# Wide products with an unread result on TensorE, around the first transposes and in the router stage of a hybrid decoder layer

## The reference, cut to what matters

```python
def decoder_layer(h, p, conv_prev, ssm_prev, prm):
    mix, ... = token_mixers(rmsnorm(h, g_mix), conv_prev, ssm_prev, prm)   # w_in, convolution, scan, chunk mix, w_out
    h = h + mix
    m = rmsnorm(h, g_moe)
    h = h + moe(m, ...)                     # 32 experts
    gate = sigmoid(rmsnorm(h, g_ple) @ w_ple_gate)
    return h + (p @ w_ple_proj) * gate, ...

def moe(x, ...):
    logits = x @ w_router + b_router
    top_v, top_i = top_k(logits, 4); gates = softmax(top_v)
    # for every expert e, on the rows that chose it:
    #   u = x[rows] @ w_up[e] + b_up[e]           1024 -> 2048
    #   act = gate * sigmoid(1.702 * gate) * (lin + 1)
    #   out[rows] += (act @ w_down[e] + b_down[e]) * g      1024 -> 1024
```

## Time and profile before

| | us |
|---|---|
| three runs, median (lowest, highest) | 1175.32 (1175.0, 1187.63) |
| profiled execution, its own time | 1171.86 |
| span of its profile | 1170.1 |
| TensorE busy | 1105.9 (95%) |
| TensorE weight loads | 454.9 (39%) |
| VectorE busy | 387.0 (33%) |
| ScalarE busy | 142.4 (12%) |
| GpSimd busy | 33.9 (3%) |
| HBM read | 429.04 MB |

### The profile page before, as it was taken

How to read it: one execution, slowest core, us unless ns; L and a number is a source line. 1 busy time by engine, 2 the same in 40 slices (tenths; PEclk the granted TensorE clock), 3 DMA queues, 4 the chain that set the end, 5 groups by cost and what they waited for, 6 DMA issues and landing times.

```text
span 1170.1 us, 16352 instructions
## 1 busy us (share of the span) xinstructions
PE 1105.9 (95%) x6482; PEld 454.9 (39%) x6482; DVE 387.0 (33%) x979; ACT 142.4 (12%) x318; POOL 33.9 (3%) x81
## 2 busy tenths in 40 slices
PE   5999999999999999989898899999989898989896
PEld 5746356333333433333333233334333333333332
DVE  3727656322222231313131122233223132222255
ACT  1322213100000100000000100001010000000022
POOL 2300021000000000000000000000000000000000
PEclk9999998999999999999999999999999999999999
DMA  8833194899999999999999999999999999999941
GB/s 285 269 148 114 42 388 182 348 429 427 428 426 426 428 428 427 429 428 428 430 427 428 427 429 426 427 428 428 428 429 428 427 428 428 429 429 429 425 179 41
DMA packets 42334, 433.88 MB, mean 371 GB/s; under 512 B 6691, under 2 KB 7851, under 8 KB 17720
## 3 DMA queue, kind: packets, MB, share of 16 engines
q1 hardware_dynamic: 40224, 428.74, 87.6%
q0 software_dynamic: 1488, 4.48, 1.1%
q10 hardware_dynamic: 584, 0.14, 0.1%
HBM read 429.04 MB, written 4.30 MB: 370 GB/s over the span
## 4 chain that ended last, share of the span: by engine, by line
PE 71%; DMA 26%; DVE 1%; ACT 1%; issue 1%; SPq 0%; DVEq 0%; ACTq 0%
PE bank L971 27%; DMA ring<-in_w_up_dram 25%; PE bank L1017 12%; PE bank L955 6%; PE bank L611 5%; PE bank L707 4%; PE bank L637 3%; PE bank L939 3%; PE bank L1001 1%; PE bank L593 1%; PE bank L1046 1%; PE bank L936 1%; PE bank L1007 1%; PE bank L870 1%; PE bank L812 1%
## 5 line engine op out<-in xcount | busy, mean ns | idle before, releaser
L971 PE MATMUL bank<-ring,aT 128*64 128x512 f32 x1536 | 350.0, 601 | 28.8 <-DMA ring<-in_w_up_dram 27.7
L971 PEld LDWEIGHTS bank<-ring,aT 128*64 128x64 f32 x1536 | 106.8, 138 | 255.7 <-issue 201.0
L1017 PE MATMUL bank<-ring,arena 128*64 128x512 f32 x768 | 169.6, 594 | 0.2
L1795 DVE TENSOR_TENSOR h<-h,bank 128x512 f32<-128x512 f32 (+1 forms) x96 | 65.7, 684 | 178.2 <-PE bank L955 175.9
L971 PE MATMUL bank<-arena,aT 128*64 128x512 f32 x512 | 115.6, 596 | 3.4 <-DMA arena<-in_w_up_dram 3.4
L1812 DVE TENSOR_SCALAR arena<-bank 128x256 f32<-128x256 f32 x64 | 27.2, 425 | 238.7 <-PE bank L971 237.4
L1821 DVE COPY aT<-bank 64x512 f32<-64x512 f32 x32 | 22.2, 694 | 245.0 <-PE bank L1017 245.0
L1271 ACT ACTIVATE arena<-arena 128x256 f32<-128x256 f32 x64 | 26.7, 417 | 548.6 <-DVE arena L1812 548.6
L1017 PEld LDWEIGHTS bank<-ring,arena 128*64 128x64 f32 x768 | 53.8, 137 | 100.9 <-issue 98.2
L955 PE MATMUL bank<-aT,arena 128*128 128x512 f32 (+1 forms) x192 | 83.5, 622 | 1.4 <-DVE aT L1821 0.9
L971 PEld LDWEIGHTS bank<-arena,aT 128*64 128x64 f32 x512 | 35.3, 136 | 77.6 <-issue 69.9
(11 more groups left out here) (313 smaller groups left out, 758.6 us busy)
## 6 DMA issues: line engine op xcount, KB each, us to landing
ring<-in_w_up_dram SPq DMA_DIRECT2D x96, 2048.0 KB, 32.6
ring<-in_w_down_dram SPq DMA_DIRECT2D x48, 2048.0 KB, 33.2
arena<-in_w_up_dram SPq DMA_DIRECT2D x32, 2048.0 KB, 33.0
arena<-in_w_down_dram SPq DMA_DIRECT2D x16, 2048.0 KB, 33.6
ring<-in_w_in_dram SPq DMA_DIRECT2D x3, 2048.0 KB, 14.1
ring<-in_w_in_dram SPq DMA_DIRECT2D x4, 1024.0 KB, 8.6
ring<-in_w_out_dram SPq DMA_DIRECT2D x1, 4096.0 KB, 13.0
ring<-in_w_ple_gate_dram SPq DMA_DIRECT2D x2, 2048.0 KB, 13.4
```

The costliest lines, as they stand in the source:

```text
L971: mm = pe.matmul(bank[n][CAP * hf:CAP * hf + CAP, :], xT[:, odd, 2 * j + a, :], up_cols(x, j, a, hf, n), start=False, stop=(j == 3 and a = ...
L1017: mm = pe.matmul(bank[4][CAP * hf:CAP * hf + CAP, :], actT[:, b, t, :], tile_of(x, UP_TILES + t)[:, 1024 * b + 512 * hf:1024 * b + 512 * h ...
L1795: tt(part, part, bank[5 + j % 2][at:at + ROWS[c], :], ALU.add).then_inc(s_free[j % 2], 1)
```

## The change

A new view `idle_rows` covers 256 float32 columns of the arena, read as 512 bf16 columns. VectorE's first instruction sets it to zero and gives `idle_ok`. A new helper `keep_clock(n, b, rows)` issues n products of a 128 by 128 bf16 stationary operand with 512 bf16 columns, each with start and stop, into bank b. No engine reads these results; where the bank is used later, its first product has start set, so it writes over them. There are 24 such products before the parameter turns, 10 before the first transposes and 2 after each of the six transposing jobs, all on zeros; then 2 before the last logits, 3 between L912 and L914, 2 before the wait for `sel0_ok` 2, and 4 after L925, on the normed rows `parts_0`. Before the first of these router groups two waits are added, for the store of the transposes of row group 1's first half and for `m1_ok` 2, which ScalarE gives when it has written those normed rows.

```diff
@@ -173,6 +173,7 @@
         bsn = view(11008, P)
         lmat = [view(3840, HEADS, P), view(15872, HEADS, P)]
         lmat_s = view(19200, HEADS, T_S)[0:T_S]
+        idle_rows = view(19200, 256).bitcast(BF16)
 
         mbf = view(0, 3072).bitcast(BF16).rearrange("p (c t n) -> p c t n", c=2, t=3)
         mbs = view(3072, 512).bitcast(BF16)
@@ -245,7 +246,7 @@
         S = semaphores(
             "a_ok ach act_ready bias_in oh_ok oh_tab aex_ok anexp a0_free a0_full a1_free a1_full bmask_ok brow_in bs_in bup_in "
             "bup_parts bup_stored cmask_ok consts conv_ok cv_out dec_in dt dt_in dtabs dtadd dtexp dtln "
-            "eac_ok end_moe fin_ss fss g_ok g_ready gex gf_in gl_ok h0_in h0t_used hf_out hfin hss ident_ok "
+            "eac_ok end_moe fin_ss fss g_ok g_ready gex gf_in gl_ok h0_in h0t_used hf_out hfin hss ident_ok idle_ok "
             "lexp m1_ok m2_ok m3_ok m_ok mask_ok mix_done mix_ok moe_done mss ngm_ok npass_ok "
             "ns_out pads par_in pb_in pch pg_sig pg_sum pp_free pp_full pr_in pt_free pt_full r1_ok rs_p_ok rso_ok sel0_ok sel_ok sig_ready sumsq tables "
             "u_in up_free up_full v_in v_out vch vgb_in vinit vn_ok w_used wmask wo_half wo_in wrt_in wrt_ok wsp_in "
@@ -578,6 +579,13 @@
                 mm.then_inc(bank_full[PS[name][0]], 1)
 
 
+            def keep_clock(n, b, rows):
+
+                for _ in range(n):
+                    pe.matmul(bank[b][:, :], rows[:, 0:P], rows[:, 0:512], start=True, stop=True)
+
+            pe.wait_ge(S["idle_ok"], 1)
+            keep_clock(24, 7, idle_rows)
             pe.wait_ge(S["ident_ok"], 1)
             pe.wait_ge(S["par_in"], 16 * 8)
             o = open_bank("par")
@@ -613,10 +621,12 @@
                         close_bank(name, mm)
                 return mm
 
+            keep_clock(10, 7, idle_rows)
             for c in range(NCH):
                 pe.wait_ge(S["xn_ok"], c + 1)
                 for hf in range(2):
                     transposed(("xT", c, hf), xn, c, 4 * hf)
+                    keep_clock(2, 7, idle_rows)
 
             for c in range(NCH):
                 for hf in range(2):
@@ -896,6 +906,10 @@
             pe.wait_ge(S["bias_in"], 32)
             up_bias(0, 0)
             turn_rows(1, (1,))
+            parts_0 = mbf[:, 0, 0, :]
+            stored(pe, ("mT", 1, 0))
+            pe.wait_ge(S["m1_ok"], 2)
+            keep_clock(2, 5, parts_0)
             logits(1)
 
             def pass_columns(d):
@@ -910,6 +924,7 @@
             for d in range(KD):
                 cols, out = pass_columns(d)
                 pe.matmul(out, h[:, 0, cols], sel_rs[:, 0, :], start=False, stop=False)
+            keep_clock(3, 5, parts_0)
             o = open_bank("pos1")
             pe.matmul(o[:, 0:NE], ones_b[0:T_S, :], m2, start=True, stop=False)
             pe.matmul(o[:, 0:NE], ones_b[:, :], m0, start=False, stop=False)
@@ -919,11 +934,13 @@
                 mm = pe.matmul(o[0:1, NE:2 * NE], ones_b[0:ROWS[c], 0:1], mask_b[0:ROWS[c], c, :],
                                start=(n == 0), stop=(n == NCH - 1))
             close_bank("pos1", mm)
+            keep_clock(2, 5, parts_0)
             pe.wait_ge(S["sel0_ok"], 2)
             for d in range(KD):
                 cols, out = pass_columns(d)
                 mm = pe.matmul(out, h[:, 1, cols], sel_rs[:, 1, :], start=False, stop=(d == KD - 1))
             mm.then_inc(S["xt_full"], 1)
+            keep_clock(4, 5, parts_0)
             for b in range(8):
                 pe.wait_ge(bank_free[b], BANK_END[1][b])
 
@@ -1368,6 +1385,7 @@
                     else:
                         step(last)
 
+            dve.memset(idle_rows, 0.0).then_inc(S["idle_ok"], 1)
             step(dve.memset(stat[:, :, :], 0.0))
             step(dve.memset(gstat[:, :, :], 0.0))
             step(dve.memset(mv[:, :, :], 0.0))
```

## The result

The changed kernel takes 1167.66 us in the median of 20 runs, the kernel before 1174.6 in the median of its 20: a ratio of 0.9943 with a 95% interval of 0.9922 to 0.9964, faster by 0.6%. The forecast was 1169.7, with a range of 1165 to 1178.5. The profiled execution took 1166.98 us (span 1165.2), 4.88 under the profiled one of before (1171.86). So the medians moved by 6.9 us and the profiles by 4.9; the experiments explain the 4.9, and the rest in part. Both kernels have single runs far above their median (up to 1189), and the ratio leaves the longest ones out.

What follows compares the result with a forecast made beforehand. The expert stretch was taken as bound by its transfer stream, whose start sets the end. Front -0.8 and router -4.8 gave -5.6 us from the profiled 1171.86, so 1166.3; plus 3.46 to the median, 1169.7, range 1165 to 1178.5.

Steps and rivals of the forecast that it cites:

- A: Issue of the first fetch that waits for an expert, at 208.51 us before; the transfer stream's start, moving the end.
- the gain is hidden anyway: Rival for the expert stretch: expert 0 starts earlier but the stream's end doesn't move, 1175.3 us; chance 0.13.
- The price of a wide product, 0.215 us: For each added 512-column bf16 product: 0.215 us at the upper clock level, 0.43 at the lower.
- The router stage, -4.8 us: Router stage with expert 0's first tile: clock held up, experts start 2.5 us earlier, first tile 2.3 us shorter.
- The front, -0.8 us: Around the first transposes: slow steps vanish, but the wait for xbc weights leaves 0.8 of 1.66 us gained.
- F: End of the last four transposes of h in the router stage; covers everything from the front to there.
- the count of slow steps: Front, 19.03 to 22.82 us: three dt and xbc steps took 3.79 us instead of 2.13, a loss of 1.66.
- the wait for the weights may bring a fall: Front: a 0.8 us wait for the xbc weights' fourth quarter may itself lower the clock, costing 1.7 us.
- The offset of 3.46 us between profile and median: Whole kernel: the median of runs stood 3.46 us above the profiled execution; kept, taking 1166.3 to 1169.7 us.
- Fillers in vain in the router stage: Rival: router fillers don't keep the clock up, the fall at 193.3 us still comes, +3.0 us, 1177.5; chance 0.20.
- The slow front: Rival in the front: products on zeros don't lift the clock, products start 9 us late, 1187.3 us; chance 0.05.
- theory A: From the narrow-products experiment in the router stage: wide column streams, not busyness, hold the clock; narrow ones cost 4 to 5 us.

Runs made afterwards that it cites:

- the router-only kernel: Changed kernel without the products on zeros and their memset, router stage's groups kept: 1170.13 us in the median of 12, ratio 0.998 to the kernel before.
- the front-only kernel: Changed kernel without the router stage's four groups and their two waits, products on zeros kept: 1171.1 us median of 13, ratio 0.998 to the kernel before.
- the late start's: Changed kernel with 24 more wide products in the router stage's last group (28 instead of 4): 1174.54 us in the median of 12.

## Why the prediction was right or wrong

**That the stream of transfers bounds the kernel and A sets the end: right.** Over fourteen profiles of ten kernels, with A from 203.0 to 233.9 us, the span less A is 961.1 to 961.8. The rival that the gain is hidden anyway falls with it. In the prediction's count of tiles, 184 by 4.9 us makes 902 us and not 897; the 896.9 us between 208.51 and 1105.43 are 4.87 a tile, and nothing else hangs on it. The first profile of before has 961.6, the highest but one, so 0.5 of the pair's 4.9 us lies behind A, in no term of the sum.

**The price of a wide product, 0.215 us: right**, in all four groups of the router stage, and partly by luck: L971, from which it was borrowed, is a float32 product with a stationary operand 64 wide (128*64), and float32 ones of full width take 0.429. On zeros in the front the ten took 2.33 us. The 24 took 6.98 and ended at 8.25, between the working's 8.1 and 9.8.

**The router stage, -4.8 us: right for this pair, too much for the kernel.** Step by step the chain came within 0.3 us of the working: L926 begins at 193.92 (said 194.16) and takes 1.91 (said 1.76), L941 begins at 197.52 (197.61) and takes 2.04 (1.76), the experts begin at 200.43 (200.2), A - F went from 17.0 to 12.6, -4.5. L759's 0.11 us a product was a little low for L912 and L925; theirs is 0.12 to 0.13. The first waiting fetch was said at 202.9 and came at 204.11, 0.8 of that from the front. But the 17.0 of the first profile was the longest of those profiled; the other profiles of kernels without the router's fillers have 15.4 to 16.0, so the stage is worth 2.9 to 4.5 us by profile, and 3.4 by the medians, which don't tell it from nothing. The mechanism stands and the size of the term was taken from one sample of a thing that varies.

**The front, -0.8 us: wrong for the pair, and too small for the medians.** F moved by +0.07. The weights' fourth quarter did bind, as the working had it, but the parameters, and so all issues behind them, landed 0.7 us later in this execution (9.46), which took up the 0.8. The medians say 2.4 us, by the router-only kernel against the changed one and by the front-only kernel against that of before; neither is clear of noise. The step that failed is the count of slow steps, taken as the 3.4 us fall of one profile. In other executions there is none, or one of 6.8 us that pushes TensorE past the landing of the weights; that profile's F is 2.5 us later. No profile with the front's products has a fall at that place except the one behind the weights' wait, which fits that they cut off the upper case. That this makes up the 2.4 us of the medians is argued, since no run of the upper half was profiled. That the wait for the weights may bring a fall was said at 1.7 us; where it came it lasted 27 us and cost some 14.

**The offset of 3.46 us between profile and median: wrong.** It was carried over to the changed kernel, which has nearly none of it: 0.7 us (1166.98 against 1167.66). That is why the measured median lies 2 us under the forecast though the sum for the profiled execution, 1166.3, was 0.7 too low: two misses of opposite sign, so the nearness of 1169.7 is in part luck. What made the offset of before isn't shown. The longer front falls, which vary by some 2.5 us, can be a part of it, but the long runs with a mean granted clock of 0.994 don't show a lower clock.

**The rivals.** Fillers in vain in the router stage: A - F is 12.6 in all six profiles that have the eleven wide ones and nothing more, so they held the clock there; in the seventh, the late start's, it fell between them. So they don't exclude the fall. The Trainium skill's page "TensorE: Matmul & The Clock Gate", in the section on why this matters for kernels, names idle gaps between bursts as what loses the clock. These traces have both: a fall right behind an idle gap (1.8 us, front only, down at 25.3 us), and falls with TensorE busy throughout, in the router stage of before (3.00 of 3.00 us ahead of 193.3). The first goes the way of that rule, the second doesn't. The slow front didn't come: the clock rose under products on zeros.

## What to carry to other kernels

When transfers bound a long stretch, find the one event that starts their steady stream; what a change before it is worth is how far it moves that event, and what doesn't move it is free. Look at the granted clock wherever TensorE does narrow products, even where it reads as fully busy; a few wide ones in waits that exist anyway pay for themselves if the work behind them was running at the lower level. And take a clock fall's price from several profiles: its place and length change from run to run, and of this change's 6.9 us 2.0 are not in the first pair of profiles.

## What the runs showed of the hardware that was not expected

- The clock was not regained by everything that is called busy: at 0.50 TensorE was busy 12.00 of 12.00 us with float32 products of 512 columns, half of them (L822) with 32 rows, and the clock stayed there for 27 us (132.2 to 159.5); in another profile for 27 us (25.3 to 52.5), much of it with steps of 8 and 288 columns, and in the late start's for 41 us (133.7 to 174.6). So a busy stream, a wide one too, doesn't always bring the upper level back as the first 24 products did in the front (6.98 us in all). It doesn't always hold it either: the fall at 132.2 us came after 2.2 us of products of 512 columns. That is against a plain reading of theory A. What began that fall and what ended these stretches the runs don't tell; it is left open.
- The granted clock of a window ahead of the first recorded change reads 1.00 though the transposes ran at the lower level: 0.231 us each against 0.109.
- Products on all-zero operands raised the clock like others: 24 in 6.98 us from a cold start, then ten in 2.33.
